# Attention values and transposed probabilities as high and low halves: three 64-column products a block of keys

## The reference

```python
s = jnp.where(valid, s + alibi, -jnp.inf)
m = jnp.max(s, axis=-1, keepdims=True)
e = jnp.exp(s - m)
l = jnp.sum(e, axis=-1, keepdims=True)
o = jnp.einsum("bhrnqk,bhrnkd->bhrnqd", e, vb) / l
```

## Time and profile before

| | |
|---|---|
| median of 3 runs | 2456.7 us |
| the profiled execution | 2454.38 us |
| its span, first to last instruction | 2452.7 us |
| mean granted TensorE clock | 0.997 |
| PE / PEld busy | 2419.0 / 2005.9 us |
| DVE / ACT / POOL busy | 1239.4 / 962.9 / 442.5 us |
| L1332, the product changed | 416 instructions of TensorE for 208 products in the program |
| attention of half 0, half 1 | some 926 to 1046 us, 1575 to 1723 us |

### The profile page before, as it was taken

The page is one execution under the profiler, slowest core; times in us unless marked ns, Lnnn a source line. Parts: engine busy times, 40 slices in busy tenths (PEclk is TensorE's granted clock), DMA queues, the critical chain, the costliest instruction groups (busy, mean ns, idle before and its releaser), DMA issues.

```text
span 2452.7 us, 31975 instructions
## 1 busy us (share of the span) xinstructions
PE 2419.0 (99%) x12800; PEld 2005.9 (82%) x12800; DVE 1239.4 (51%) x2012; ACT 962.9 (39%) x1503; POOL 442.5 (18%) x605
## 2 busy tenths in 40 slices
PE   8999999999999999999999999999999999999997
PEld 7888888888888888888888877888788888888886
DVE  6353334673555534468845475445453536433334
ACT  6332223432333224645434343487253434322222
POOL 1442000201222221122112242332020012100001
PEclk9999999999999999999999999999999999999998
DMA  7644333535322235344344341664343244533331
GB/s 218 195 153 130 95 95 98 161 92 166 95 61 69 70 103 145 114 166 127 87 119 140 93 127 60 166 144 103 123 130 110 86 146 163 172 95 103 95 95 69
DMA packets 333522, 293.04 MB, mean 119 GB/s; under 512 B 14528, under 2 KB 272832, under 8 KB 332864
## 3 DMA queue, kind: packets, MB, share of 16 engines
q1 hardware_dynamic: 297856, 204.56, 28.1%
q0 software_dynamic: 34336, 86.18, 11.6%
q10 hardware_dynamic: 1184, 0.27, 0.1%
HBM read 257.34 MB, written 33.62 MB: 119 GB/s over the span
## 4 chain that ended last, share of the span: by engine, by line
PE 96%; DVE 1%; ACT 1%; issue 1%; POOL 0%; DMA 0%; SPq 0%; DVEq 0%; ACTq 0%; POOLq 0%
PE acc L1066 18%; PE acc L1068 18%; PE acc L1067 18%; PE acc L1092 10%; PE acc L1094 10%; PE acc L1093 10%; PE side L1332 2%; PE side L1147 1%; PE side L1390 1%; PE side L1256 1%; PE side L1313 1%; PE side L1227 1%; PE side L1239 1%; PE side L1293 0%; PE side L1160 0%
## 5 line engine op out<-in xcount | busy, mean ns | idle before, releaser
L2051 DVE TENSOR_TENSOR w_lo<-w_raw,w_hi 128x1024 fp32r<-128x1024 f32 x384 | 474.1, 1235 | 526.1 <-ACT w_hi L1569 524.3
L1569 ACT ACTIVATE w_hi<-w_raw 128x1024 fp32r<-128x1024 f32 x384 | 405.8, 1057 | 557.4 <-PE acc L1094 314.6
L1066 PE MATMUL acc<-ha_hi,w_hi 128*128 128x512 f32 (+1 forms) x960 | 380.8, 397 | 0.0
L1066 PE MATMUL acc<-hb_hi,w_hi 128*128 128x512 f32 x960 | 373.6, 389 | 0.0
L1068 PE MATMUL acc<-hb_hi,w_lo 128*128 128x512 f32 x960 | 373.5, 389 | 0.0
L1067 PE MATMUL acc<-hb_lo,w_hi 128*128 128x512 f32 x960 | 373.4, 389 | 0.0
L1068 PE MATMUL acc<-ha_hi,w_lo 128*128 128x512 f32 (+1 forms) x960 | 368.6, 384 | 0.0
L1067 PE MATMUL acc<-ha_lo,w_hi 128*128 128x512 f32 (+1 forms) x960 | 367.7, 383 | 0.0
L1092 PE MATMUL acc<-w_hi,act_hi 128*128 128x512 f32 x688 | 273.8, 398 | 0.0
L1094 PE MATMUL acc<-w_lo,act_hi 128*128 128x512 f32 x688 | 268.4, 390 | 0.0
L1093 PE MATMUL acc<-w_hi,act_lo 128*128 128x512 f32 x688 | 268.1, 390 | 0.0
(11 more groups left out here) (405 smaller groups left out, 3378.3 us busy)
## 6 DMA issues: line engine op xcount, KB each, us to landing
w_raw<-in_ffn_w_gate SPq DMA_DIRECT2D x88, 512.0 KB, 3.7
w_raw<-in_ffn_w_up SPq DMA_DIRECT2D x88, 512.0 KB, 3.7
w_raw<-in_ffn_w_down SPq DMA_DIRECT2D x88, 512.0 KB, 3.4
w_raw<-in_w_in SPq DMA_DIRECT2D x56, 512.0 KB, 3.8
x_dram<-xbuf POOLq DMA_DIRECT2D x24, 512.0 KB, 3.0
xbuf<-x_dram POOLq DMA_DIRECT2D x24, 512.0 KB, 6.2
w_raw<-in_w_out SPq DMA_DIRECT2D x16, 512.0 KB, 3.5
w_raw<-in_mem_wq SPq DMA_DIRECT2D x16, 512.0 KB, 4.0
```

The costliest lines, as they stand in the source:

```text
L1066: pe.matmul(out, hi[:, k, 0:m], xh[:, k, 0:n], start=(k == 0), stop=False)
L1569: act.activation(w_hi[:, j % RING, :], w_raw[:, j % RING, :], ACT.Copy).then_inc(w_hi_ok, 1)
L2051: dve.tensor_tensor(w_lo[:, j % RING, :], w_raw[:, j % RING, :], w_hi[:, j % RING, :].bitcast(F32), ALU.subtract).then_inc(w_lo_ok, 1)
```

## The change

The values are written as a pair: ACT rounds all four tiles to float32r (`v_hi_ok`), DVE subtracts. Each goes to `v_dram` beside the other, channels of one head together, and `v_load` brings one head at a time, in a row of 64 high and 64 low channels. `pt_copy` writes one buffer `pt_hi` in float32r and waits first for the product that read it; a new DVE step `pt_low` subtracts it from PSUM into `pt_lo` and now gives `pT_sbuf`. `pv` makes three float32r products for each block of keys where one float32 product stood. The slots of the value tiles are used twice, tiles 2 and 3 after tiles 0 and 1.

```diff
-KV_PARTS = [("c", 2, 1, "d"), ("r", 4, TT, "adad")]
+KV_PARTS = [("c", 2, 1, "d"), ("r", 4, TT, "dddd")]
...
-        v_dram = scratch("v_dram", (HALVES, TT, P, AH * AD))
+        v_dram = scratch("v_dram", (HALVES, TT, P, AH, 2, AD), F32R)
...
-        def pt_of(n):
-            return arena[:, 8 + n % 2, :]
+        pt_hi, pt_lo = arena_r[:, 8, :], arena_r[:, 9, :]
...
-                eng.wait_ge(slot_stored[k], 16 * (5 * h + uses))
+                eng.wait_ge(slot_stored[k], 16 * (6 * h + uses))
...  POOL
-                if n >= 8:
-                    pool.dma_start(v_dram[h][n - 8], v_slot(h, n - 8)).then_inc(slot_stored[n - 8], 16)
-                    return
                 for part in range(2):
-                    dst = (q_dram if n < 4 else k_dram)[h][part][n % 4]
-                    pool.dma_start(dst, qk_slot(h, n, part)).then_inc(slot_stored[2 * (n % 2) + part], 16)
+                    src = qk_slot(h, n, part)
+                    if n >= 8:
+                        dst, src = v_dram[h][n - 8][:, :, part, :], src.rearrange("p (h d) -> p h d", h=AH)
+                    else:
+                        dst = (q_dram if n < 4 else k_dram)[h][part][n % 4]
+                    pool.dma_start(dst, src).then_inc(slot_stored[2 * (n % 2) + part], 16)
...
-                        if u in (9, 17):
+                        if u > 4 and u % 4 == 1 and u // 4 + 1 < AH:
                             pool.wait_ge(attn["out_psum"], h * UNITS + u - 1)
-                            v_load(h, u // 8 + 1)
+                            v_load(h, u // 4 + 1)
...  TensorE, pv
                     for a, values in enumerate(groups):
+                        out = SB[3][:, out_cols(n, a)]
                         for c, v in enumerate(values):
-                            mm = pe.matmul(SB[3][:, out_cols(n, a)], pt_of(n)[:, (2 * a + c) * P:(2 * a + c + 1) * P], v,
-                                           start=(c == 0), stop=(c == len(values) - 1))
+                            keys = slice((2 * a + c) * P, (2 * a + c + 1) * P)
+                            v_high, v_low = v[:, 0:AD], v[:, AD:2 * AD]
+                            pe.matmul(out, pt_hi[:, keys], v_high, start=(c == 0), stop=False)
+                            pe.matmul(out, pt_hi[:, keys], v_low, start=False, stop=False)
+                            mm = pe.matmul(out, pt_lo[:, keys], v_high, start=False, stop=(c == len(values) - 1))
...  ACT
-                rgroup(4, TT, sub, lambda tt: v_slot(h, tt), before=lambda tt: slot_free(act, h, tt, 4))
+                rgroup(4, TT, sub, lambda tt: qk_slot(h, 8 + tt, 0), high=v_hi_ok,
+                       before=lambda tt: slot_free(act, h, 2 * (tt % 2), 4 + tt // 2))
...
-                    act.activation(pt_of(n)[:, 0:m], SB[2][:, 0:m], ACT.Copy).then_inc(attn["pT_sbuf"], 1)
+                    if n:
+                        act.wait_ge(attn["out_psum"], n)
+                    act.activation(pt_hi[:, 0:m], SB[2][:, 0:m], ACT.Copy).then_inc(attn["pT_high"], 1)
...  DVE
+                def low(tt, turn, val):
+                    dve.wait_ge(v_hi_ok, TT * h + tt + 1)
+                    slot_free(dve, h, 2 * (tt % 2) + 1, 4 + tt // 2)
+                    dve.tensor_tensor(qk_slot(h, 8 + tt, 1), A[turn % NBANK][:], qk_slot(h, 8 + tt, 0).bitcast(F32),
+                                      ALU.subtract).then_inc(acc_dve, 1)
...
+                def pt_low(u):
+                    n = h * UNITS + u
+                    m = TOK if h else (u % TT + 1) * P
+                    dve.wait_ge(attn["pT_high"], n + 1)
+                    dve.tensor_tensor(pt_lo[:, 0:m], SB[2][:, 0:m], pt_hi[:, 0:m].bitcast(F32), ALU.subtract).then_inc(attn["pT_sbuf"], 1)
...
                         if u >= 1:
                             fin(u - 1)
+                        if 0 <= u < UNITS:
+                            pt_low(u)
```

More of the change, by code:

```diff
@@ L366, in hybrid_layer @@
         qk_hi_ok = sem("qk_hi_ok")
+        v_hi_ok = sem("v_hi_ok")
         slot_stored = [sem(f"slot_stored{k}") for k in range(4)]
@@ L385, in hybrid_layer @@
             "distance", "log_count", "qk_in0", "qk_in1", "v_in0", "v_in1", "bias_in0", "bias_in1", "scores", "max",
-            "neg_max", "probs", "pT_psum", "pT_sbuf", "out_psum", "out_sbuf", "outT_psum", "outT_sbuf",
+            "neg_max", "probs", "pT_psum", "pT_high", "pT_sbuf", "out_psum", "out_sbuf", "outT_psum", "outT_sbuf",
             "k_class", "stat_out", "stat_in", "merge_diff", "merge_exp", "out_merged", "outT_sum")}
@@ L778, in qk_load, with v_load @@
                         pool.dma_start(queries(h, hd, b)[rows, :], q_dram[h][(a + b) % 2][p][ch, :]).then_inc(s, 16)
-            def v_load(h, p):
-                s = attn["v_in0"] if p % 2 == 0 else attn["v_in1"]
+            def v_load(h, hd):
+                s = attn["v_in0"] if hd % 2 == 0 else attn["v_in1"]
                 for hh in range(h + 1):
                     first = TT - 1 if h and hh == 0 else 0
-                    pool.dma_start(v_ring(h, p)[:, hh * TT + first - (TT - 1) * h:(hh + 1) * TT - (TT - 1) * h, :],
-                                   v_dram[hh][first:, :, p * P:(p + 1) * P].rearrange("i p d -> p i d")).then_inc(s, 16)
+                    pool.dma_start(v_ring(h, hd)[:, hh * TT + first - (TT - 1) * h:(hh + 1) * TT - (TT - 1) * h, :],
+                                   v_dram[hh][first:, :, hd].rearrange("i p a d -> p i (a d)")).then_inc(s, 16)
                     if h:
-                        rows = v_dram[hh].rearrange("i p d -> (i p) d").rearrange("(c r) d -> c r d", r=TT)
-                        pool.dma_start(vs_ring(p)[:, hh, :, :], rows[:, :, p * P:(p + 1) * P]).then_inc(s, 16)
+                        rows = v_dram[hh].rearrange("i p h a d -> (i p) h (a d)").rearrange("(c r) h d -> c r h d", r=TT)
+                        pool.dma_start(vs_ring(hd)[:, hh, :, :], rows[:, :, hd, :]).then_inc(s, 16)
             def bias_load(h, hd):
@@ L1323, in pv @@
                     pe.wait_ge(attn["pT_sbuf"], n + 1)
-                    if u % 8 == 0:
-                        pe.wait_ge(attn["v_in0"] if p % 2 == 0 else attn["v_in1"], 32 * h + (64 if h else 16) * (p // 2 + 1))
+                    if i == 0:
+                        pe.wait_ge(attn["v_in0"] if hd % 2 == 0 else attn["v_in1"], 64 * h + (64 if h else 16) * (hd // 2 + 1))
                     if h == 0:
-                        groups = [[v_ring(h, p)[:, c, ch] for c in range(i + 1)]]
+                        groups = [[v_ring(h, hd)[:, c, :] for c in range(i + 1)]]
                     else:
-                        groups = [[v_ring(h, p)[:, i + c, ch] for c in range(2)], [vs_ring(p)[:, c, i, ch] for c in range(2)]]
+                        groups = [[v_ring(h, hd)[:, i + c, :] for c in range(2)], [vs_ring(hd)[:, c, i, :] for c in range(2)]]
                     for a, values in enumerate(groups):
+                        out = SB[3][:, out_cols(n, a)]
                         for c, v in enumerate(values):
-                            mm = pe.matmul(SB[3][:, out_cols(n, a)], pt_of(n)[:, (2 * a + c) * P:(2 * a + c + 1) * P], v,
-                                           start=(c == 0), stop=(c == len(values) - 1))
+                            keys = slice((2 * a + c) * P, (2 * a + c + 1) * P)
[3 more added lines that the diff above has]
+                            mm = pe.matmul(out, pt_lo[:, keys], v_high, start=False, stop=(c == len(values) - 1))
                     mm.then_inc(attn["out_psum"], 1)
@@ L1623, in some @@
                         for tt in cut[s]:
-                            if before and EV[BANK[i] + tt][0] == "a":
+                            if before and (high or EV[BANK[i] + tt][0] == "a"):
                                 before(tt)
@@ L2201, in kv_in @@
                 qk_blocks(h, 6, 8, sub)
-                def put(tt, turn, val):
-                    if EV[turn][0] == "d":
-                        slot_free(dve, h, tt, 4)
-                    copy_out(turn, val, v_slot(h, tt))
-                rgroup(4, TT, sub, put)
+                def low(tt, turn, val):
[3 more added lines that the diff above has]
+                                      ALU.subtract).then_inc(acc_dve, 1)
+                rgroup(4, TT, sub, low)
             def norm(r, q):
```

20 lines of the change are left out of this document (8 added, 12 removed).

## The result

The changed kernel takes 2491.03 us (median of four runs, 2489.43 to 2492.75) against 2456.47 for the kernel before: a ratio of 1.0142, 95% interval 1.0125 to 1.016. The forecast was 2494, own range 2486 to 2503. Executions of the kernel before fall on two levels, near 2454.5 us at a mean granted clock of 0.997 and near 2456.5 at 0.996, so differences under 2 us are not told apart here. The profiled execution took 2491.06 us with a span of 2489.3, 36.6 us more than the 2452.7 before; the sum of the prediction was 37.5.

A forecast was written before the change was run, and what follows sets the result against it. TensorE, busy 99% of the span, was taken as the bound. Terms 22.9 + 7.5 + 6.1 + 1.0 = 37.5 us on 2454.4 gave 2491.9, stated as 2494 since the profiled execution was 2.3 below the median; own range 2486 to 2503.

The forecast's parts named there:

- The bound: Whole kernel: TensorE, busy 99% of the span, pays for all it issues; other engines cost only where it waits.
- The product, 22.9 us: Attention's probabilities-times-values product: 208 more TensorE instructions at 0.11 us each, 8.8 us in half 0, 14.1 in half 1.
- The bounds of 0.13 and 0.03: Limits for one 64-column float32r product in us: 0.13 gives +35 in all, 0.03 (columns alone count) gives -27.
- rival 3: Attention product: one-pass products hold TensorE under 0.073 us, so the kernel gets faster, 2440 us; chance 0.04.
- Waits of half 0, 6.1 us: Attention of half 0 from 978 us: twelve TensorE ticks wait 0.2 to 0.86 us for DVE's subtraction.
- Waits of half 1, 7.5 us: Attention of half 1: TensorE waits for DVE's subtraction and late ACT copies, 3.0 + 1.1 + 0.7 + 0.4 + 0.97 + 1.35.
- ACT's late place: Half 1, where ACT has 7.67 us of own work between copies: its copy also waits for the product, 0.97 us more once.
- What should be seen: Profile after: 624 products 0.11 us apart, some 13 us of TensorE waits at transposes, ACT's idle time ended by the products.
- The values, 1.0 us: Value staging: reused slots hold ACT and DVE until stores land, delaying the "ab" chain; 1 us, range 0 to 5.
- 1, only the products: Attention: the waits for DVE don't come and only the products cost, 2480 up to 2484 us; chance 0.18.
- 2, ACT as the bound: Half 1: ACT's copy waits for the product each tick and can't catch up, 2503 to 2514 us; chance 0.18.
- 3 and 4: Attention product: 3, short one-pass products, 2440 us, chance 0.04; 4, no change, 2452 to 2462 us, chance 0.03.

The follow-up runs named there:

- run 6: Changed kernel with its handover kept, but one float32 product of the high parts per key block instead of three float32r ones: 2472.1 us.
- run 8: On top of run 7, the two products of the high probabilities made one with 128 columns, DVE adding the two column groups: 2464.1 us, ratio 1.0034.
- run 5: Changed kernel with three products, all of the copied probabilities, two places for them, no DVE subtraction, old handover: 2475.62 us, ratio 1.0082.
- run 1: Changed kernel without its middle product (high probabilities times low values), two instructions a key block: 2472.05 us, ratio 1.0068.
- run 2: Changed kernel with DVE's output copy and subtraction of low probabilities ahead of its softmax step: 2485.11 us.
- run 4: Changed kernel with high probabilities alternating between two places, so ACT's copy waits for the products of two units before: 2485.02 us.
- run 10: On top of run 7, ACT's copy of the transposed probabilities placed ahead of its exp: 2477.6 us.
- run 3: Changed kernel with the old staging of values put back: four slots, whole float32r stores, no low part of the values: 2489.96 us.
- run 11: One 128-column float32r product a key block, high probabilities alone, two places, no subtraction; against the kernel before: 2442.33 us, ratio 0.9951.
- run 9: On top of run 8, ACT's copy of the transposed probabilities placed ahead of its exp: 2460.97 us, ratio 1.0026.
- run 7: Changed kernel with DVE's subtraction ahead of its softmax step and two places for the high probabilities: 2477.08 us.

## Why the prediction was right, step by step

**The bound.** Right. Whatever TensorE issued more it paid for, and work of the others cost where TensorE came to wait.

**The product, 22.9 us.** Right in its price: starts 0.11 us apart, and run 6 has a float32 pass and a float32r product equal in every tick of half 1 to 0.04 us. The bounds of 0.13 and 0.03 can be dropped, and with them rival 3. The guess behind it, that at few columns the number of instructions counts and not their columns, is borne out for 64 and 128 columns by run 8 (0.22 us a pair). The Trainium skill, "TensorE: Matmul & The Clock Gate", section "Weight-path perf modes", turns Fast Weight Load on for 128 weights if the input type is not FP32. The loads of the new float32r products show no sign of it: their median is 192 ns, as that of the float32 loads in the kernel before. But a product's price is not what it costs or gives back. Alone, 208 of them added 21.1 us (run 5), 19.7 by the medians, as some of them filled old waits; taken away from a kernel whose waits for ACT they filled, they gave 19.0 (run 1). In the sum the term was 1 to 2 us too large, because it took no count of the waits that longer products fill.

**Waits of half 0, 6.1 us.** Right: the stretch grew by 14.2, and by 8.15 with the passes alone, so 6.05. Against the ticks of run 5 ten are later by 0.25 to 0.89 us, where I had twelve by 0.2 to 0.86. The tick at 1008.53 waits 2.93 - 2.40 = 0.53, forecast 0.57.

**Waits of half 1, 7.5 us.** The stretch grew by 22.7, of it 13.0 with the passes alone: 9.7. Starts of TensorE's ticks there, from the two timelines:

| places | before | after | less 0.44 for the products | forecast |
|---|---|---|---|---|
| four short ticks | 3.21, 3.19, 3.19, 3.19 | 4.39, 4.40, 4.35, 4.36 | 0.72 to 0.77 | 0.74 |
| twelve long ticks | 3.86 to 3.91 | 4.35 to 4.50 | 0 to 0.20, together 1.0 | 0.07, sixteen times |
| first tick (no products) | 2.28 | 2.83 | 0.55 (nothing taken off) | 0.7 |
| ACT's late place | 5.36 | 6.73 | 0.93 | 0.97 |
| the tick behind it | 3.81 | 5.23 | 0.98 | 0 |
| three later places | 3.89, 3.89, 3.90 | 4.70, 4.70, 4.70 | 0.36 to 0.37 | 0.45 |

Each term stands, but the sum lacked one: the tick behind the longest wait, in which TensorE ran at half clock. Its natural length is that of a short tick, 3.65 us, so the clock took 1.6. Against the kernel before it looks like 0.98 only, because that kernel had a wait in this tick which the prediction passed over, as the list puts it down to "issue":

```profile
1605.14 0.47 PE L1297 MATMUL side<-k_asis,q_asis 128*128 128x256 f32 x2 [0.42 <-issue]
```

By the code these score products wait for ACT's reordering of the queries (L1805), and that ended at 1605.05. By the starts they stand 0.6 us later than in the next tick. In the passes alone most of this wait is filled (the tick takes 3.83), and so is 0.9 us of the old one in the late place. The 2.2 us between 9.7 and 7.5 are these 0.9 and what the tick behind takes over run 5, 5.23 - 3.83 = 1.4.

That the waits come from DVE's order, run 2 shows: 3.63 and 4.33 us a tick with the subtraction ahead. That ACT's wait for the products is a second cause, run 4 shows: 6.0 us, where my terms have 0.97 + 1.35 for half 1 and nothing for half 0. In half 0 I gave all waits to DVE's place; 1.6 us of them were ACT's (run 4). With both edits and ACT's copy ahead (run 10) the kernel is 2.0 us over the passes alone, so little is left that these two causes and ACT's order don't cover.

**What should be seen.** The idle time of ACT before its copy, ended by the products, in half 1 (us, times, longest):

```profile
ACT arena_r L1834 <- PE side L1337: 35.9, 21, 5.8
```

Waits at the transposes were to be some 13 us, by the list; the list has 8.8, by the ticks it is nearer 14 (6.05 + 9.7, less 1.4 for the clock). I had called my mechanism wrong if they came under 5 us or were ended by ACT. Neither came: 4.0 us are ended by DVE, 3.8 are put down to issue and 1.0 is ended by ACT. Still, a number from the list of waits was the wrong thing to name, as the list leaves out what a held weight load costs.

**The values, 1.0 us.** Right in the place, too large in size. Up to the first transposes the changed kernel needs 1.1 us more, and run 3 as a whole 1.1 less, but both are under what can be told apart. The traces show one wait that belongs to the values, and it is where I put it, in the chain of "ab": TensorE waits 0.4 us at L1349 for DVE's last small step (L2485). The kernel before and run 3 don't have it, and run 3 is 0.35 us earlier at the first transposes. So 0.4 us is shown; what the other 0.7 up to there is stays open, and run 3 has it too. The stores held DVE and ACT up by 5.0 and 4.9 us, and slack took the rest. The Trainium skill, "DMA: Bandwidth & Descriptors", section "Specifications", wants at least 512 bytes a transfer for line rate, and I had taken the upper end of my range, 5 us, for that case; run 3 doesn't bear such a price out. The stores of 256 bytes did land later in part, after 2.8 to 6.4 us where the whole rows of the kernel before took 2.3 to 4.5, but the ones over 3.7 us were the last two of each half, and no wait is ended by them.

**From 2491.9 to 2494.** The profiled execution of before was 2.3 us under its median, and I added that. That median is of the upper of the two levels of the kernel before, while the changed kernel's median is its profiled time. The sum alone was 0.9 high, and the addition made it 3. That the sum came so near is in part luck: the 2.2 us too few in half 1 are set off by 1.8 too many for the products and by the 1.4 at the end, for which the sum had no term.

**Rivals.** 1, only the products: 2475.62 is what they and the values cost alone; the changed kernel is 15.4 over it. 2, ACT as the bound: it would have made 2503 or more; ACT stood idle 35.9 us before its copies in half 1. It is the bound only at the late place, at three later ones and at three ticks of half 0, and these took back 4 us of the gain in run 1, 5 or more in run 8 and more than half of what is missing in run 11. 3 and 4 are out by the 0.11 us between the products and by run 6.

## What to carry to other kernels

A step that moves the handover to another engine has to be placed in that engine's order. Behind a step that itself waits for the end of the tick, it sets a floor under every tick (here 4.39 us); in front of it the floor is gone (3.63), and only the four places where ACT is late grew, by 0.05 to 0.14 us. The price of instructions on the bounding engine is taken back wherever that engine already waits for something else, so cost and gain are both to be worked out tick by tick. With 64 or 128 columns, fewer instructions count here and not fewer columns.

## What I had not expected of the hardware

A single wait of TensorE can cost more than its length. Behind the late place the granted clock fell to 0.50, its lower level, in eight of the thirteen profiles. The cost is what the ticks behind it took over their natural length (3.65 us for the tick right behind with three products a block, 3.20 with two instructions; in run 9 less a wait of 0.66 us that it holds):

| idle time of TensorE, us | profile | cost, us |
|---|---|---|
| 2.2, 2.6, 2.7, 2.1 | changed kernel, runs 1, 6, 9 | 1.6 each |
| 2.3, 2.2, 3.0 | runs 2, 3, 8 | 3.1 to 3.2 each |
| 1.4 | run 7 | 6.4 |
| 1.3, 0.9, 0.4, 1.2, 2.2 | kernel before, runs 4, 5, 10, 11 | none, clock 1.00 |

The kernel before isn't free of it either. Some 27 us behind its last transposes of attention TensorE waits 2.2 us for DVE (`hb_lo`), and so it does in every kernel here. First the products behind that wait in the kernel before, then in run 11:

```profile
1746.42 0.50 PE L1092 MATMUL acc<-w_hi,hb_hi 128*128 128x512 f32 x1 [2.24 <-DVE hb_lo L2499]
...
1747.43 0.63 PE L1092 MATMUL acc<-w_hi,hb_hi 128*128 128x512 f32 x1
1735.86 0.50 PE L1094 MATMUL acc<-w_hi,hb_hi 128*128 128x512 f32 x1 [2.23 <-DVE hb_lo L2507]
...
1736.66 0.40 PE L1094 MATMUL acc<-w_hi,hb_hi 128*128 128x512 f32 x1
```

From the end of this wait to the transposes of `res_cz` ten profiles take 77.8 to 77.9 us, with products 0.43 us apart for a while, and three (runs 9, 10 and 11, the third group) take 76.3, with the clock at 1.00 in the stretch behind the wait. It is the same wait of 2.2 us with the same work behind it, so the length of the wait alone doesn't decide; what does is open. The profiles of before and after both have this stretch, so it doesn't touch their difference. The 1.6 us that it costs are near the 2 us between the levels of the kernel before; that they are its cause isn't shown.
